# Whole-page loads in the compression block and batched 16-bit routing in a decoder step on one core

## What is computed

```python
def compress(raw, pe, w1, w2):
    B, S = raw.shape[:2]
    n = S // CMP_BLOCK
    x = raw.reshape(B, n, CMP_BLOCK, 2, N_KV, HEAD_DIM) + jnp.transpose(pe, (1, 0, 2))[:, :, None, :]
    x = jnp.transpose(x, (0, 1, 3, 4, 2, 5)).reshape(B, n, 2, N_KV, CMP_BLOCK * HEAD_DIM)
    hdn = jax.nn.gelu(jnp.einsum('bnsgf,sfh->bnsgh', x, w1))
    return jnp.einsum('bnsgh,shd->bnsgd', hdn, w2)
```

```python
    s = jax.nn.sigmoid(h.astype(jnp.float32) @ router_w.astype(jnp.float32))
    grp = (s + router_b.astype(jnp.float32)).reshape(N, N_GROUPS, EXPERTS_PER_GROUP)
    g_sel = jnp.argmax(lax.top_k(grp, 2)[0].sum(-1), axis=-1)
    ...
    counts = jnp.bincount(flat_e, length=N_EXPERTS)
    padded = (counts + MOE_BLOCK - 1) // MOE_BLOCK * MOE_BLOCK
    pad_end = jnp.cumsum(padded)
    pad_start = pad_end - padded
    start = jnp.cumsum(counts) - counts
    dest = pad_start[e_sorted] + jnp.arange(A, dtype=jnp.int32) - start[e_sorted]
```

## Time and profile before

| | us |
|---|---|
| median of 3 runs | 1498.45 (1494.69 to 1502.95) |
| profiled execution, its time | 1498.93 |
| its span, first to last instruction | 1496.8 |
| TensorE matmul busy | 1282.4 (86%) |
| VectorE busy | 742.0 (50%) |
| ScalarE busy | 528.9 (35%) |
| GpSimd busy | 108.5 (7%) |

### The profile page before, as it was taken

One profiled execution on the slowest core, in us unless ns is written; L12 is line 12 of the kernel. 1 busy time (PEld: TensorE's weight loads), 2 busy tenths in 40 slices (PEclk: granted clock), 3 DMA queues, 4 the chain that ended last, 5 costly groups with the idle time before them and its releaser, 6 DMA issues. The chain is left out here.

```text
span 1496.8 us, 21480 instructions
## 1 busy us (share of the span) xinstructions
PE 1282.4 (86%) x7890; PEld 929.3 (62%) x7891; DVE 742.0 (50%) x1547; ACT 528.9 (35%) x873; POOL 108.5 (7%) x159
## 2 busy tenths in 40 slices
PE   4289999999538989999997999279999999999962
PEld 1156666665326556656666887167788887788731
DVE  0012222221212545656676666768856658675248
ACT  0010000100000137755555221157646457665132
POOL 1000011000000000000000000001101001110040
PEclk9599999999757559999999999569999999999986
DMA  9753345500432063000003332559976769975572
GB/s 328 237 162 137 134 162 90 97 12 12 100 88 81 14 213 126 2 1 1 2 2 103 112 118 106 191 185 371 375 261 240 268 245 362 376 248 207 204 285 94
DMA packets 100626, 237.69 MB, mean 159 GB/s; under 512 B 19914, under 2 KB 27525, under 8 KB 100391
## 3 DMA queue, kind: packets, MB, share of 16 engines
q1 hardware_dynamic: 88951, 196.47, 39.3%
q0 software_dynamic: 8144, 27.62, 5.1%
q10 hardware_dynamic: 3456, 12.58, 2.1%
HBM read 198.61 MB, written 40.13 MB: 159 GB/s over the span
## 5 line engine op out<-in xcount | busy, mean ns | idle before, releaser
L2079 PE MATMUL psum<-w_hi,x_parts 128*128 128x512 f32 x736 | 240.3, 398 | 8.4 <-DVE x_parts L2198 7.5
L2191 DVE TENSOR_TENSOR w_lo<-raw,w_hi 128x2048 fp32r<-128x2048 f32 x96 | 215.6, 2288 | 56.8 <-ACT w_hi L2138 56.7
L2138 ACT CAST w_hi<-raw 128x2048 fp32r<-128x2048 f32 x96 | 178.5, 1912 | 93.5 <-DVE work L2209 50.6
L592 PE MATMUL psum<-low,high 128*128 128x512 f32 (+5 forms) x576 | 200.3, 502 | 0.0
L2079 PEld LDWEIGHTS psum<-w_hi,x_parts 128*128 128x128 f32 x736 | 139.9, 190 | 39.9 <-issue 11.0
L592 PEld LDWEIGHTS psum<-low,high 128*128 128x128 f32 (+1 forms) x576 | 105.4, 188 | 77.5 <-issue 66.9
L2079 PE MATMUL psum<-w_lo,x_parts 128*128 128x512 f32 x368 | 144.6, 393 | 0.0
L1501 DVE CUSTOM_DVE_ANT_0 low<-psum,high 128x512 f32<-128x512 f32 (+3 forms) x160 | 88.8, 593 | 78.1 <-PE psum L1341 77.8
L2079 PE MATMUL psum<-w_hi,a_parts 128*128 x368 | 121.2, 401 | 5.6 <-DVE a_parts L2204 5.5
L1469 ACT ACTIVATE low<-low,high 128x640 f32<-128x640 f32 (+7 forms) x128 | 93.0, 729 | 51.4 <-DVE high L1501 51.4
L1664 PE MATMUL psum<-wo_parts,mix_parts 128*128 128x512 f32 (+1 forms) x432 | 104.0, 398 | 6.8 <-DVE wo_parts L1801 6.2
(11 more groups left out here) (310 smaller groups left out, 1519.9 us busy)
## 6 DMA issues: line engine op xcount, KB each, us to landing
raw<-in_moe_w_gate SPq DMA_DIRECT2D x16, 2048.0 KB, 11.2
raw<-in_moe_w_up SPq DMA_DIRECT2D x16, 2048.0 KB, 12.0
raw<-in_moe_w_down SPq DMA_DIRECT2D x16, 2048.0 KB, 11.2
high<-in_w_mod SPq DMA_DIRECT2D x12, 2048.0 KB, 13.9
y_d<-work ACTq DMA_DIRECT2D x24, 512.0 KB, 7.0
high<-in_x_prompt SPq DMA_DIRECT2D x16, 512.0 KB, 3.9
y_d<-high SPq DMA_DIRECT2D x1, 8192.0 KB, 37.3
low<-in_w_in SPq DMA_DIRECT2D x3, 2048.0 KB, 15.1
```

Of the source, the lines that this page charges most:

```text
L592: mm = pe.matmul(c.bank(2 + n % 2)[0:T, 0:w], hT[i % 2][:, k, 0:T], c.w_in[:, k, a:a + w], start=(k == 0), stop=(k == KT - 1))
L2079: mm = pe.matmul(out, left[l][:, k * P:(k + 1) * P], w[:, bass.ds(at + k * step, 512)], start=n == 0, stop=n == len(steps) - 1)
L2138: act.copy(c.w_hi[:, at:at + PART // 2], c.raw[:, o:o + PART // 2]).then_inc(hi_done[p], 1)
L2191: dve.tensor_tensor(c.w_lo[:, at:at + PART // 2], c.raw[:, o:o + PART // 2], c.w_hi[:, at:at + PART // 2].bitcast(F32), ALU.subtract).then ...
```

## The change

In the compression block, a page or prompt tile is loaded as it lies, each pair of rows as one run of 2 KB per partition: one DMA for a prompt tile, one for a page, into 8 buffers. ScalarE copies each tile into one of two buffers `pairs`, in the order that the transposes read. w2 and then w1 are loaded from ScalarE's queue at the block's start. `xcT` is laid out by pair k first, so that the additions on VectorE read PSUM with a step of 16 elements and the products read 192 columns in a row.

In the routing block, the constants come in two DMAs, and the first steps do not wait for them; several waits between independent VectorE instructions are gone. The membership matrices and the counts are bfloat16, with integers up to 128 or multiples of 128, which are exact; the token number is the sum of two products (row, and tile times 128), added at the end. The prefix over tiles is done by 8 further matmuls onto the same bank, with a shifted view of counts that has zeros ahead. The 36 membership instructions become four large ones. The routing weights and the final destinations are computed at the end, behind the token numbers.

```diff
@@ block_compression
-    xcT = c.view(W_, 4, NPAIR)
+    xcT = c.view(W_, 2, CB // 2, 2 * nblk)
+    NAT = 8
+    nat = [c.view(KVR_ + 1024 + 512 * s, 2, 4, HD) for s in range(NAT)]
+    pairs = [c.view(KVR_ + 512 * s, 4, 2, HD) for s in range(2)]
@@ sync
-                if n >= 3:
-                    sp.wait_ge(nt_ps, n - 2)
+                if n >= NAT:
+                    sp.wait_ge(paired, n - NAT + 1)
-                    src = t["o_cmp_p"][0, 0, n * 256:(n + 1) * 256].rearrange("(p q) s g d -> p q (s g) d", q=2)
-                    for q in range(2):
-                        sp.dma_start(dst[:, :, q, :], src[:, q]).then_inc(nat_in[n % 3], 16)
+                    src = t["o_cmp_p"][0, 0, n * 256:(n + 1) * 256].rearrange("(p q) s g d -> p (q s g d)", q=2)
+                    sp.dma_start(dst, src).then_inc(nat_in[n % NAT], 16)
-                        src = t["cache_cmp_kv"][0, bass.ds(page, 1)].rearrange("n (p q) s g d -> p q (n s g) d", q=2)
-                        for q in range(2):
-                            sp.dma_start(dst[64 * pg:64 * pg + 64, :, q, :], src[:, q]).then_inc(nat_in[n % 3], 16)
-                if n == 3:
-                    sp.dma_start(w1, t["cmp_w1"][0].rearrange("s (c p) h -> p s c h", p=P)).then_inc(cw_in, 16)
-                    sp.dma_start(w2, t["cmp_w2"][0].rearrange("s h d -> h s d")).then_inc(cw_in, 16)
+                        src = t["cache_cmp_kv"][0, bass.ds(page, 1)].rearrange("n (p q) s g d -> p (n q s g d)", q=2)
+                        sp.dma_start(dst[64 * pg:64 * pg + 64, :], src).then_inc(nat_in[n % NAT], 16)
@@ tensor
-                pe.wait_ge(nat_in[n % 3], need[n])
+                pe.wait_ge(paired, n + 1)
-                                      nat[n % 3][:, sg, :, :].rearrange("p q d -> p (q d)"), c.ident)
+                                      pairs[n % 2][:, sg, :, :].rearrange("p q d -> p (q d)"), c.ident)
-                    cols = xcT[:, 2 * s:2 * s + 2, :].rearrange("p g (n c) -> p g n c", c=CB // 2)[:, :, :, k]
-                    mm = pe.matmul(c.bank(2 + s)[:, 0:2 * nblk].rearrange("p (g n) -> p g n", g=2), w1[:, s, k, :], cols,
+                    mm = pe.matmul(c.bank(2 + s)[:, 0:2 * nblk], w1[:, s, k, :], xcT[:, s, k, :],
@@ scalar
+            act.dma_start(w2, t["cmp_w2"][0].rearrange("s h d -> h s d")).then_inc(cw_in, 16)
+            act.dma_start(w1, t["cmp_w1"][0].rearrange("s (c p) h -> p s c h", p=P)).then_inc(cw_in, 16)
+            for n in range(tiles):
+                act.wait_ge(nat_in[n % NAT], need[n])
+                if n >= 2:
+                    act.wait_ge(nt_ps, n - 1)
+                act.copy(pairs[n % 2], nat[n % NAT].rearrange("p q a d -> p a q d")).then_inc(paired, 1)
@@ vector
-                            xcT[:, 2 * s + g, n * P:(n + 1) * P].rearrange("p (n c) -> p n c", c=CB // 2),
-                            c.bank(n % 2)[:, (2 * s + g) * P:(2 * s + g + 1) * P].rearrange("p (n c) -> p n c", c=CB // 2),
-                            peT[:, s, :].unsqueeze(1).to_broadcast([P, 8, CB // 2]), ALU.add)
+                            xcT[:, s, :, g * nblk + 8 * n:g * nblk + 8 * n + 8],
+                            c.bank(n % 2)[:, (2 * s + g) * P:(2 * s + g + 1) * P].rearrange("p (n c) -> p c n", c=CB // 2),
+                            peT[:, s, :].unsqueeze(2).to_broadcast([P, CB // 2, 8]), ALU.add)
@@ block_routing, sync and vector
-            sp.dma_start(consts, t["cph4"]).then_inc(c.cph_in, 16)
+            sp.dma_start(keys, t["cph4"][:, 0:rest]).then_inc(keys_in, 16)
+            sp.dma_start(consts, t["cph4"][:, rest:]).then_inc(consts_in, 16)
-            dve.wait_ge(c.cph_in, 48)
-            tt(a4, x[:, :, :, 0], x[:, :, :, 1], ALU.max)
+            dve.tensor_tensor(a4, x[:, :, :, 0], x[:, :, :, 1], ALU.max)
...
+            dve.wait_ge(consts_in, 16)
+            dve.tensor_copy(strict_h, strict).then_inc(cnt_ready, 1)
             dve.wait_ge(cnt_ps, 1)
-            linked(dve.tensor_copy(tot, c.bank(1)[:, 0:NT * NE].rearrange("p (i e) -> p i e", i=NT)))
-            for i in range(NT):
-                tt(pref[:, i + 1], pref[:, i], tot[:, i], ALU.add)
+            linked(dve.tensor_reduce(totals, c.bank(1)[:, 0:NT * NE].rearrange("p (i e) -> p e i", i=NT), AX.X, ALU.add))
...
-            for i in range(NT):
-                T = tile_rows(i)
-                for k in range(2):
-                    dve.tensor_scalar(one_place[0:T, 2 * i + k], place_n[0:T], place_f[0:T, i, k:k + 1], None, ALU.is_equal)
-                    ins = dve.tensor_scalar(one_slot[0:T, 2 * i + k], slot_n[0:T], slot_f[0:T, i, k:k + 1],
-                                            tok_id[0:T, i:i + 1], ALU.is_equal, ALU.mult)
+            tt(same_slot, slot_n.unsqueeze(1).to_broadcast([P, 2 * NT, n_slot]),
+               over_last(slot_f.rearrange("p i k -> p (i k)"), n_slot), ALU.is_equal)
+            dve.tensor_tensor(one_place, place_n.unsqueeze(1).to_broadcast([P, 2 * NT, P]),
+                              over_last(place_f.rearrange("p i k -> p (i k)"), P), ALU.is_equal)
+            dve.tensor_scalar(one_slot[:, :, 0, :], same_slot, row, None, ALU.mult)
+            dve.tensor_tensor(one_slot[:, :, 1, :].rearrange("p (i k) q -> p i k q", k=2),
...
@@ tensor
-            pe.matmul(c.bank(0)[:, 0:NT * NE], strict, flat, start=True, stop=True)
-            pe.matmul(c.bank(1)[:, 0:NT * NE], ones, flat, start=True, stop=True).then_inc(cnt_ps, 1)
+            pe.matmul(c.bank(1)[:, 0:NT * NE], ones_h, flat, start=True, stop=True).then_inc(cnt_ps, 1)
+            pe.matmul(c.bank(0)[:, 0:NT * NE], strict_h, flat, start=True, stop=False)
+            for n in range(1, NT):
+                mm = pe.matmul(c.bank(0)[:, 0:NT * NE], ones_h, padded[:, pad - n * NE:pad - n * NE + NT * NE], start=False,
+                               stop=n == NT - 1)
-                mm = pe.matmul(c.bank(2)[:, 0:MAX_SLOTS + 1], one_place[0:T, n], one_slot[0:T, n], start=n == 0, stop=n == 2 * NT - 1)
+                mm = pe.matmul(c.bank(2)[:, 0:2 * (MAX_SLOTS + 1)], one_place[0:T, n],
+                               one_slot[0:T, n].rearrange("p a q -> p (a q)"), start=n == 0, stop=n == 2 * NT - 1)
```

More of the change, by code:

```diff
@@ L1828, in new @@
         return v if len(dims) == 1 else v.rearrange("p (a b) -> p a b", a=dims[0])
-    strict, key16, key4, limits, before, slot_n, tok_id, place_n = (
-        new(*d) for d in ((P,), (NE,), (4,), (8,), (NE, NE), (MAX_SLOTS + 1,), (NT,), (P,)))
-    consts = c.scratch[:, 0:off[0]]
-    s, grp, y, y2, tmp, oh1, oh2, m, dest = (new(NT, NE) for _ in range(9))
+    key16, key4, limits = new(NE), new(4), new(9)
+    keys = c.scratch[:, 0:off[0]]
+    rest = off[0]
+    strict, before, place_n, tile_at, row = new(P), new(NE, NE), new(P), new(NT), new(1)
@@ L1835, in block_routing @@
+    consts = c.scratch[:, rest:off[0]]
+    s, grp, y, y2, dest = (new(NT, NE) for _ in range(5))
+    ohs, tmp = new(2 * NT, NE), new(2 * NT, NE)
+    oh1, oh2 = ohs[:, 0:NT], ohs[:, NT:]
     a4, b4, c4, d4, m1g, e4, f4, m2g, gs, gk, gsel, pen = (new(NT, 4) for _ in range(12))
-    r1, r2, w1, w2, ws = (new(NT) for _ in range(5))
-    pref, tot = new(NT + 1, NE), new(NT, NE)
-    ones, over, nb, starts, tri = new(P), new(NE, 8), new(NE), new(NE), new(NE, NE)
+    r1, r2, ws = (new(NT) for _ in range(3))
@@ L1839, in block_routing @@
+    ww = new(2, NT)
+    totals, over, nb, starts, slots, tri = new(NE), new(NE, 9), new(NE), new(NE), new(NE), new(NE, NE)
     table, exps, ends = new(MAX_SLOTS, NE), new(MAX_SLOTS), new(NE + 1)
     dests, slot_f, place_f = (new(NT, 2) for _ in range(3))
-    one_place, one_slot = new(2 * NT, P), new(2 * NT, MAX_SLOTS + 1)
-    assert off[0] <= 9216
-    sg, cnt_ready, cnt_ps, dest_ready, ids_ps, tab_ready, link = (
-        sem(n) for n in ("sig_ready", "cnt_ready", "cnt_ps", "dest_ready", "ids_ps", "tab_ready", "r_link"))
+    same_slot, rows = new(2 * NT, MAX_SLOTS + 1), new(MAX_SLOTS + 1)
```

117 lines of the change are left out of this document (68 added, 49 removed).

## The result

The changed kernel took 1450.41 us (median of 4 runs, 1444.92 to 1455.30) where the kernel before, on the same chip, took 1499.91 (1494.69 to 1502.95): a ratio of 0.9673, with a 95% interval of 0.9626 to 0.9719, some 49 us less. The profiled execution took 1448.43 us, its span is 1446.3, 50.5 less than before.

The account below looks back on a forecast made before the run. Barriers end each block; SyncE's issuing bounds the compression fill, strided reads its products, a VectorE chain the routing. Savings 25.4 + 7.9 + 11.8 = 45.1 us, from the median 1498.45 and profiled 1498.93, gave 1453.5 us; range 1442 to 1466.

Parts of the forecast that it names:

- The bound: Compression fill stage: SyncE's issuing of 32 small DMAs, one per 1.07 us, sets the time, not bandwidth.
- Spacing of the pages: Compression fill: sixteen whole-page DMAs 1.10 us apart, last issue at 416.2; part of 25.4 us saved.
- Landing and w1: Compression fill: pages land 2.3 us after issue; w1 on ScalarE's queue has 25 us to land, cost nothing.
- Rival 1: Compression fill: w1 shares transfer engines with the prompt tiles, 4.3 us less gain, 1458 us; 12 in 100.
- The Trainium skill's rule on issuers: Compression fill: another issuer saves only issuing time on the same 16 engines; cited as partly supporting w1 delaying prompt tiles.
- 6.4 us of the weight loads: Compression fill: moving w1 and w2 off SyncE, which they held from 401.3 to 407.7, saves 6.4 us.
- The ScalarE copy: Compression fill: new 128x512 copy per tile, about 0.6 us, costing only its one pass at the end.
- Products: Compression products: contiguous columns take 13.2 us against 21.1, 7.9 saved; bounds 10.5 at full clock, 0.5 at half.
- Rival 2: Compression products keep their 21 us, stride not the cause or clock not rising; 1461 us; 14 in 100.
- Routing: Routing block: shorter VectorE chain, four membership instructions, 18 16-bit matmuls; 11.8 us saved, range 10.9 to 12.8.
- The first expert's weights: End of routing: last weights land 18.6 us after issue, one more small DMA adds 0.4; in time by 4 us.
- Rival 3, the clock in the prompt attention,: Prompt attention: clock rise shifted 20 us either way moves the time 10 us, 1443 or 1464; 14 in 100.

Follow-up runs that it names:

- the first of these runs: Changed kernel with each cache tile's second page loaded from GpSimd's queue and w1 issued behind the fourth tile's copy; 1451.26 us.
- the second: Changed kernel with second pages on GpSimd's queue, w1 at the block's start, next block's constants and window rows held until the last tile is copied; 1444.97 us.
- queue_only: Kernel before with only w2 and w1 moved to ScalarE's queue at the compression block's start; 1502.32 us.
- four orders tried here: Changed kernel as it stands, with w1 late, and with GpSimd as second page issuer, w1 late or window rows late; fill 27.5 to 29.0 us.

## Why the prediction was right

The forecast was 1453.5 us; 1450.4 was measured. That the sum is near is in part luck: the errors of the stages (2.9 us too much, 1.0 and 1.7 too little) cancel to 0.2 us, and the remaining distance is within what the attention's clock does from one execution to the next. Of the three things that the prediction said would show it wrong, two came: the third and fourth prompt tile landed at 405.0 and 407.2, after 405, and the prompt attention's clock rose 12.3 us after its start and not 29.9. The third, contiguous columns at 0.3 us at full clock, did not. Step by step:

- **The bound.** Right. SyncE's issues held the fill stage; with half of them and the weights elsewhere it lost 22.5 us, and giving 16 of them back cost 10 (two issues per page).
- **Spacing of the pages.** A term too small. I took 1.10 us from the selection cache; measured 1.23, since one issue takes 0.47 us here and 0.34 there. So the last issue came at 417.2, and not at 415.4 (the predicted 416.2, less the 0.8 us by which the block began sooner). That is 1.8 us of the 2.9 us missing in this stage. The prompt tiles' four DMAs took 1.96 us instead of 2.5.
- **Landing and w1** ("cost taken as nothing"). With 2.3 us to land and 2.8 us for the last tile, 417.2 gives 422.3; the products began at 423.4. So the landings cost the other 1.1 us of the 2.9: the last page took 2.7 us to land, 0.4 more than the row, and its tile then stood behind four that had piled up, some 0.7 us. Rival 1's mechanism was there, and the third and fourth tile were as late as it had them (405 and 407), but not its 4.3 us: w1 late brought no time. The cover named in the prediction, SyncE's slow issuing, held for the most part.
- **The Trainium skill's rule on issuers.** The page "DMA: Bandwidth & Descriptors" of the Trainium skill, section "Issuing engines are not separate DMA queues", says that DMAs of another issuer run on the same 16 engines, and that only the time to issue is saved. By that rule GpSimd as second issuer can bring issuing time and no more, and the trace agrees: SyncE's issuing of the pages fell from 18.97 to 9.22 us in the first of these runs, and the fill took 27.6 us, and 29.0 in the second. In queue_only not even the time to issue was saved (53.8). The sum of the prediction took the 6.4 us of the weight loads as saved; that came true only together with the longer runs.
- **The ScalarE copy** 0.62 us (0.6 taken), hidden but for its pass at the end. The strided additions 0.88 us for four, as before: the rule on lines ("SBUF — State Buffer" of the Trainium skill, section "Door 1: The DMA port swizzle"), weighed in the prediction, does not show for VectorE. For TensorE's strided operand no run separates it from another cause.
- **Products.** 0.33 and 0.166 us at the two clocks, as taken (0.33 and 0.165), and the full clock 3.3 us after the start and not 5.4: 8.9 us saved, not 7.9. When the clock rises differs from one execution to the next (10.7 to 13.5 us in nine profiles), so that the term was near is luck in part. Rival 2 fell; the strided layout took 21.1 us, mostly at full clock. The lower bound of 0.5 us saved at half clock does not follow from the prediction's own 0.33 us for each of 64 products: that is 21.1 us, nothing saved.
- **Routing.** The membership matrices were ready 18.5 us after the block's start (18.8 predicted). The 16-bit matmuls were below my lower bound: 0.072 us each, bounds 0.11 to 0.223. That is what was mis-sized: the middle of the bounds put 3.0 us in the sum, the matmuls took 1.29, and what remained on the path was the slot table, 2.3 us behind the memberships. The moved weight steps took 1.8 us, not 2.3. The stated ends of the block (970.4 and 972.3) are 0.3 us less than their terms add up to. Together 13.5 us, not 11.8, above the range of 10.9 to 12.8.
- **The first expert's weights** in time, as costed: the last landed at 928.6, before the next block's 931.48, with 2.8 us to spare where I had 4.
- **Rival 3, the clock in the prompt attention,** came true beside the forecast, by 6.6 us of the 10 it allowed, and not as an effect of the change. Its price was too high: a rise t us later was to cost t/2, but 17.6 us sooner gave 6.6 us and 3.8 us later (the second profile of after) cost 1.6, some 0.4 t. The range held it. The second profiled execution of before took 1486.75 us, 12 less than the first: 6.5 us less in the attention, 3.7 in the experts and 2.3 before the compression block. From it the same sum would have started 12 us lower; the median of several runs is the better base where two levels occur.

## What to carry to other kernels

When a stage waits for many small paged loads, look at how far apart the issuing engine's DMAs are before thinking of bandwidth: one DMA per page, laid down as it lies in memory and rearranged by an idle engine, with the weights on another queue, took a 51 us stage to 28.6. After that, in the four orders tried here, the arrivals were the bound, and a second issuer or another order only moved the wait. Lay out a matmul's moving operand contiguously: the strided one took 0.33 us at either clock, the contiguous one 0.33 and 0.166; and before a gain in an untouched block is believed, profile the same program twice.

## What was not expected of the hardware

- With a 2.1 MB load on another queue, eight DMAs in 64-float runs took 10.69 us to issue and not 5.05: five took 0.42 to 0.51 us each as before, the last three 2.1 to 3.1. Issuing is not independent of what is under way.
- A half page of 64 KB landed 2.3 us after its issue began at a DMA share of 0.48, a page of 128 KB after 7.0 us in the median at 0.87, and the last page, with w1 in, after 2.7.
- 16-bit matmuls of 66 columns with new weights each ran 0.072 us apart at half clock (18 in 1.29 us), those of 144 columns 0.145 (8 in 1.16 us), while one pass of a 32-bit one in the same block took 0.23 with either.
- A program that is not changed rises to the full clock in the same block 12 us after its start in one execution and 30 or 34 us in another, with 6 to 9 us of difference in the stage, though TensorE was busy for 29.76 of the 29.9 us before the late rise.
